# A two-block transformer kernel on one core: the first block's work in a new order, the modulation fetched and multiplied by halves

## The reference, cut to what matters

```python
mod = jax.nn.silu(c) @ w_mod[l] + b_mod[l]            # c: 1 x 1024, w_mod: 1024 x 6144
sh_m, sc_m, gt_m, sh_f, sc_f, gt_f = jnp.split(mod, 6)
h = rms_norm(x, g_mix_norm[l]) * (1.0 + sc_m) + sh_m
q_a, k_a, v_a, q_i, k_i, w_i, q_b, k_b, v_b, gate_a, gate_b = jnp.split(h @ w_in[l], split_at)
o_a = dsa_attention(q_a, k_a, v_a, q_i, k_i, w_i)     # 64 keys of each query by index scores
o_b = moba_attention(q_b, k_b, v_b)                   # causal, one block of 256
merged = sigmoid(gate_a) * (o_a @ w_br_dsa[l]) + sigmoid(gate_b) * (o_b @ w_br_moba[l])
x = x + gt_m * (merged @ w_out[l])
h = rms_norm(x, g_ffn_norm[l]) * (1.0 + sc_f) + sh_f
g_ff, u_ff = jnp.split(h @ w_gate_up[l], 2)
x = x + gt_f * ((silu(g_ff) * u_ff) @ w_down[l])
```

## Time and profile before

| | |
|---|---|
| median of three runs | 1673.88 us |
| the profiled execution's own time | 1669.84 us |
| its span | 1668.0 us |
| mean granted clock of TensorE | 0.945 |
| TensorE busy | 1498.2 us (90%) |
| DVE busy | 844.6 us (51%) |
| ACT busy | 690.7 us (41%) |
| read from HBM | 268.15 MB |
| chain that ended last: TensorE, DVE, ACT, DMA | 78%, 9%, 5%, 3% |

### The profile page before, as it was taken

How to read it: one execution, slowest core, us unless ns; L and a number is a source line. 1 busy time by engine, 2 the same in 40 slices (tenths; PEclk the granted TensorE clock), 3 DMA queues, 4 the chain that set the end, 5 groups by cost and what they waited for, 6 DMA issues and landing times.

```text
span 1668.0 us, 17947 instructions
## 1 busy us (share of the span) xinstructions
PE 1498.2 (90%) x6942; PEld 1194.7 (72%) x6942; DVE 844.6 (51%) x1011; ACT 690.7 (41%) x864; POOL 34.2 (2%) x52
## 2 busy tenths in 40 slices
PE   4989896769999999999899999799997777899998
PEld 2757664558887788877688887678885664588886
DVE  1465573545455554554755445544545336555453
ACT  2334343333433534444344444644433345553442
POOL 0010000000000000000000001000000010000000
PEclk9899998879999999999899999989999777999999
DMA  8654553535655556544456564535655230055552
GB/s 305 205 190 132 209 177 126 169 109 177 190 188 177 174 180 191 187 146 157 160 170 200 176 202 140 194 101 184 191 181 175 81 127 1 1 170 184 187 191 76
DMA packets 187879, 270.10 MB, mean 162 GB/s; under 512 B 8350, under 2 KB 134118, under 8 KB 187816
## 3 DMA queue, kind: packets, MB, share of 16 engines
q1 hardware_dynamic: 186660, 267.08, 48.8%
q10 hardware_dynamic: 996, 1.88, 0.3%
q0 software_dynamic: 160, 0.26, 0.2%
HBM read 268.15 MB, written 1.05 MB: 161 GB/s over the span
## 4 chain that ended last, share of the span: by engine, by line
PE 78%; DVE 9%; ACT 5%; DMA 3%; issue 3%; SPq 0%; POOL 0%; POOLq 0%; ACTq 0%; DVEq 0%
PE bank L1561 23%; PE bank L1563 23%; PE bank L1562 23%; DVE w_lo_ring L1125 2%; DMA raw_ring<-in_w_in_dram 2%; ACT w_hi_ring L832 2%; PE bank L1591 2%; PE bank L1695 1%; PE bank L1663 1%; PE bank L1748 1%; DVE arena L1413 1%; DMA glu_s<-in_cmp_pos_dram 1%; DMA raw_ring<-in_w_br_moba_dram 1%; PE bank L1824 1%; DVE arena L1397 1%
## 5 line engine op out<-in xcount | busy, mean ns | idle before, releaser
L1125 DVE TENSOR_TENSOR w_lo_ring<-raw_ring,w_hi_ring 128x2048 fp32r<-128x2048 f32 (+1 forms) x231 | 525.4, 2277 | 548.3 <-ACT w_hi_ring L1081 361.4
L1561 PE MATMUL bank<-w_hi_ring,h_hi 128*128 128x512 f32 (+2 forms) x1392 | 560.1, 402 | 2.7 <-issue 2.2
L1563 PE MATMUL bank<-w_hi_ring,h_lo 128*128 128x512 f32 (+2 forms) x1392 | 548.2, 394 | 0.0
L1562 PE MATMUL bank<-w_lo_ring,h_hi 128*128 128x512 f32 (+2 forms) x1392 | 547.9, 394 | 0.0
L1081 ACT ACTIVATE w_hi_ring<-raw_ring 128x2048 fp32r<-128x2048 f32 x158 | 302.5, 1915 | 322.4 <-PE bank L1563 320.2
L1561 PEld LDWEIGHTS bank<-w_hi_ring,h_hi 128*128 128x128 f32 x1392 | 270.0, 194 | 66.1 <-issue 13.1
L1563 PEld LDWEIGHTS bank<-w_hi_ring,h_lo 128*128 128x128 f32 x1392 | 268.2, 193 | 56.4
L1562 PEld LDWEIGHTS bank<-w_lo_ring,h_hi 128*128 128x128 f32 x1392 | 269.5, 194 | 51.3
L832 ACT ACTIVATE w_hi_ring<-raw_ring 128x2048 fp32r<-128x2048 f32 (+1 forms) x73 | 136.5, 1876 | 180.8 <-PE bank L1563 113.5
L1561 PE MATMUL bank<-w_hi_ring,f_hi 128*128 128x512 f32 x440 | 171.9, 391 | 7.5 <-DVE f_lo L1519 7.5
L1563 PE MATMUL bank<-w_hi_ring,f_lo 128*128 128x512 f32 x440 | 171.5, 390 | 0.0
(11 more groups left out here) (228 smaller groups left out, 877.3 us busy)
## 6 DMA issues: line engine op xcount, KB each, us to landing
raw_ring<-in_ffn_w_gate_up_dram SPq DMA_DIRECT2D x176, 512.0 KB
raw_ring<-in_ffn_w_down_dram SPq DMA_DIRECT2D x44, 1024.0 KB
raw_ring<-in_w_in_dram SPq DMA_DIRECT2D x22, 1024.0 KB
raw_ring<-in_w_gate_up_dram SPq DMA_DIRECT2D x44, 512.0 KB
raw_ring<-in_w_mod_dram SPq DMA_DIRECT2D x18, 1024.0 KB
raw_ring<-in_w_down_dram SPq DMA_DIRECT2D x11, 1024.0 KB
raw_ring<-in_conv_w_in_dram SPq DMA_DIRECT2D x16, 512.0 KB
arena<-in_w_mod_dram SPq DMA_DIRECT2D x6, 1024.0 KB, 16.0
```

The costliest lines, as they stand in the source:

```text
L1125: dve.tensor_tensor(w_lo[:, u % RING, 0:words], raw[:, r % RING, 0:words], w_hi[:, u % RING, 0:words].bitcast(F32), ALU.subtract).then_inc ...
L1561: pe.matmul(dst, hi, whi, start=start, stop=False)
L1562: pe.matmul(dst, hi, wlo, start=False, stop=False)
L1563: return pe.matmul(dst, lo, whi, start=False, stop=stop)
```

## The change

Nothing of the computation is left out. The plan's items stand in a new order, and some are cut in two:

- *Modulation by halves.* A half row is an item of its own (`mod_row(m, half)`): TensorE multiplies one half into one bank, ACT copies the first half to `acc`, DVE adds the second to it (a new instruction). The two halves are fetched and multiplied around one unit, so that a unit, a half, a unit and a half follow each other in the ring, and a half frees its slot when TensorE has done it. The sum stands right behind the second half.
- *h in two halves.* Chunks 2 and 0 (halves of scale and shift for tiles 0 to 3) come first, `mod_a` works by halves, and unit 0 (qi, first half) runs before chunks 3 and 1 are multiplied. The gain rows are issued by ACT's queue behind x.
- *Evacuations behind their units.* Most of them stand right behind the unit that ends the product, where they stood behind the next unit. ki comes after qi. Index products are inside three units instead of two.
- *Dsa's attention in three units instead of four*, with half of the transposes of o ahead of gb's last unit, and the sigmoid behind the others.
- *moba's branch first, products by chunk*: bb 0, ba 0, bb 1, ba 1 (moba's output stands in tiles 0 to 3 now); the first half of merged is transposed before ba 1, whose unit is done one tile of tokens after the other (`by_token_tile`), the second half inside out1. out1's last unit is done that way too.
- *Mod chunk 11 at the end*: it is fetched during out1 and multiplied behind it, before x is scaled; the four `normf` groups and unit 31 (first of the feed-forward) are interleaved.

```diff
+    def by_token_tile(stage, chunk, number, parts, between=()):
+        u = len(units)
+        units.append((stage, chunk, number))
+        for tt in range(TT):
+            add("lin", stage=stage, chunk=chunk, part=number, parts=parts, unit=u, sub=tt, subs=TT, by_tt=True)
+            add("evac", stage=stage, chunk=chunk, tt=tt)
+            if tt == 0:
+                plan.extend(between)
+        add("then split", unit=u)
...
-    part("qa", 0, 0, 2, [evac("ga", 1), mod_row(7), topk(0, 2), topk(0, 3)])
-    part("qa", 0, 1, 2, [mod_sum(7), mod_load(8), topk(1, 0)])
+    part("qa", 0, 0, 2, [mod_row(7, 0), mod(7, 1), topk(1, 0)])
+    part("qa", 0, 1, 2, [mod_row(7, 1), mod_sum(7), evac("qa"), mod(8, 0)])
...
+    part("out1", 1, 0, 2, [mod(11, 1)])
+    by_token_tile("out1", 1, 1, 2)
+    add("square")
+    plan.extend(mod_rows(11) + mod_sum(11))
+    add("scale_x", norm=1)
...
+    def transfer(*entry):
+        r = number("early") if entry[0] == "mod" and entry[1] in EARLY_MODS else EARLY + number("ring")
+        raw[r] = entry
+        issue.append(r)
+        return r
...
+    freed = {r: ("raw_done", e[1] + 1) if e[0] == "unit" else ("t_done", find["tg", "mrow", (e[2], e[1])] + 1) for r, e in raw.items()}
...
+                    if st == "mrow" and item["c"]:
+                        dve.wait_ge(sem("t_done"), tg + 1)
+                        wait_group(dve, find["tg", "mrow", (0, g)])
+                        a = acc[:, item["of"] % 2, :]
+                        dve.tensor_tensor(a, b[:, :], a, ALU.add).then_inc(free, 1)
...
                     elif st == "mod":
-                        wait_group(pe, find["tg", "mrow", g])
+                        wait_group(pe, find["tg", "mrow", (1, g)])
```

More of the change, by code:

```diff
@@ L124, in lin_out @@
         units.append((stage, 1, 0))
[L125 to L132, removed]
+        by_token_tile(stage, 1, 1, 2, between=tgroup("norm", 2, norm=then))
     def nsa_attention():
@@ L231, in make_plan @@
-    add("mod_a", norm=0)
+    plan.extend(mod_rows(0) + mod_sum(0))
+    add("mod_a", norm=0, half=0)
+    plan.extend(tgroup("normf", 4, norm=0)[:2])
     add("then split", unit=-RING)
-    plan.extend(tgroup("normf", 2, norm=0))
-    add("then split", unit=1 - RING)
-    plan.extend(tgroup("normf", 4, norm=0)[2:])
[L236 to L244, removed]
+    plan.extend(mod_load(3) + mod_load(1))
+    add("lin", stage="qi", chunk=0, part=0, parts=2, unit=0, sub=0, subs=1)
+    units.append(("qi", 0, 0))
+    plan.extend(mod_rows(3) + mod_sum(3) + mod_rows(1) + mod_sum(1))
@@ new lines, in make_plan @@
+    add("mod_a", norm=0, half=1)
+    plan.extend(tgroup("normf", 4, norm=0)[2:])
+    add("then split", unit=3 - RING)
+    part("qi", 0, 1, 2, [evac("qi"), mod(4, 0)])
+    part("ki", 0, 0, 1, [mod_row(4, 0), evac("ki"), mod(4, 1)])
+    part("qb", 0, 0, 2, [mod_row(4, 1), mod_sum(4), tgroup("ki", 1), mod(5, 0)])
+    part("qb", 0, 1, 2, [tgroup("qi", 2), evac("qb"), mod_row(5, 0), mod(5, 1)])
+    part("kb", 0, 0, 2, [mod_row(5, 1), mod_sum(5), mod(6, 0)])
+    part("kb", 0, 1, 2, [tgroup("qb", 2), evac("kb"), mod_row(6, 0), mod(6, 1)], [index[0], [], index[1], index[2]])
@@ L270, in make_plan @@
-    plan.extend(evac("bb", 1))
-    add("mod_a", norm=1)
-    plan.extend(tgroup("merged", 4))
-    for c in range(2):
-        lin("out1", c, 2)
-    norm(1, False)
-    ffn(0, "f0", 1, then=2)
+    part("ga", 0, 0, 2, [topk(0, 0)], inside[0])
+    part("ga", 0, 1, 2, [evac("ga"), topk(0, 1)], inside[1])
+    part("ga", 1, 0, 2, [topk(0, 2)], inside[2])
+    part("ga", 1, 1, 2, [evac("ga", 1), topk(0, 3), mod(7, 0)], inside[3])
+    part("qa", 0, 0, 2, [mod_row(7, 0), mod(7, 1), topk(1, 0)])
+    part("qa", 0, 1, 2, [mod_row(7, 1), mod_sum(7), evac("qa"), mod(8, 0)])
@@ new lines, in make_plan @@
+    part("gb", 1, 0, 2, [tgroup("o", 4)[:2]], inside[2])
+    part("gb", 1, 1, 2, [evac("gb", 1), tgroup("o", 4)[2:]])
+    add("sigmoid")
+    part("bb", 0, 0, 1, [mod(10, 0)])
+    part("ba", 0, 0, 1, [evac("bb", 0), mod_row(10, 0), mod(10, 1)])
+    part("bb", 1, 0, 1, [evac("ba", 0), mod_row(10, 1), mod_sum(10), evac("bb", 1), tgroup("merged", 4)[:2]])
+    add("mod_a", norm=1, half=0)
+    by_token_tile("ba", 1, 0, 1)
+    part("out1", 0, 0, 2, inside=[tgroup("merged", 4)[2:], []])
+    part("out1", 0, 1, 2, [evac("out1", 0), mod(11, 0)])
@@ L277, in make_plan @@
+    part("out1", 1, 0, 2, [mod(11, 1)])
[3 more added lines that the diff above has]
+    add("scale_x", norm=1)
+    plan.extend(tgroup("normf", 4, norm=1)[:2])
+    add("gu", unit=len(units), sub=0)
+    plan.extend(tgroup("normf", 4, norm=1)[2:])
+    add("gu", unit=len(units), sub=1)
+    units.extend([("f0", 0, 0), ("f0", 0, 1)])
+    ffn(0, "f0", 1, then=2, begun=True)
     begin_glu("f1", 2)
@@ L331, in make_plan @@
     for item in plan:
-        if item["kind"] == "lin" and item["unit"] == 0:
-            split(RING - 1)
         if item["kind"] == "then split":
@@ L444, in two_block_program @@
 def two_block_program(nc, A, out):
[L445 removed]
+    plan, units, raws, issue, unit_raw, find, pair_after, freed = make_plan()
     def rows(w):
```

168 lines of the change are left out of this document (75 added, 93 removed).

## The result

The changed kernel takes 1680.07 us (median of 11 runs, 1674.39 to 1682.87) against 1673.88 for the kernel before (11 runs, 1669.98 to 1676.51): 0.35% slower, ratio 1.0035 with a 95% interval of 1.0023 to 1.0047. The forecast was 1673.5, no change; the measured time lies 6.6 above it, at the upper edge of the forecast's own stretch of 1667 to 1680.

What follows compares the result with a forecast made beforehand. TensorE, busy for 90% of the span, was taken as the bound, so only its waits and low clock could be won back. Terms summed to -0.4 us on the profiled 1669.84, 4.0 below the median: 1673.5, range 1659 to 1687.

Steps and rivals of the forecast that it cites:

- both mechanisms that were to eat the gain: Mod-row sums wait for adds behind low splits (+3.9, +4.9); updates after out1 wait behind a split needing row 11 (+10.4).
- dsa: Attention in three units instead of four: same matmuls with the waits nearer, +0.2 us, bounds -2 and +4.
- start to ki's end: From the start through ki: unit 0 starts earlier, at 31.7 instead of 36.3, then loses its lead; +1.9 us.
- units 3 to 8: Half mod rows make sums wait for adds behind low splits, with some lower clock: 19.9 against 16.0, +3.9 us.
- moba: The moba attention stretch keeps its places: 0 us.
- the next six units: The six units after moba: waits for adds in front of sums, 14.2 against 9.3, +4.9 us.
- o transposes to the end of out1: Waits behind the sigmoid and for merged go, new waits of 9.3 come, mod row 11 moves out: -21.7 us.
- end of out1 to the second unit: Out1's end to the second feed-forward unit: updates wait behind a split whose transfer needs row 11's first half; +10.4 us.
- rival 2: The low clock lasts behind waits for sums, each costing 5 to 6 instead of 2.5: 11 more, 1684.5 us; 15%.
- Rival 3: The start gains nothing: shared rings land the gain rows at 16.1 again, unit 0 at 36.3; +4.6, 1678.1 us; 8%.
- row 6 is the exception: Mod row 6 meets the index scores: kb's rope and unit 9's split stand ahead of index product 3 on DVE; 7.3 us.
- Rival 1: DVE reaches each add a microsecond earlier, so waits stay short and the clock up: 13 less, 1660 us; 27%.

Runs made afterwards that it cites:

- e3_rows_sp: The changed kernel with the seven small transfers of gains back on SP behind the first two 1 MB transfers: 1682.65 us, 1.0046 against the kernel before.
- e2_tail: The changed kernel with mod row 11's halves and sum and the splits of units 32 and 33 rearranged around out1's end: 1665.64 us.
- e6_dsa4: e4_both with dsa's attention over four units instead of three and the four o transposes behind the last: 1639.83 us, 0.9794 against the kernel before.
- e5_before_sig: The kernel before with only the sigmoid moved behind the o copies: 1669.54 us, 0.9976 against the kernel before.
- e4_both: The changed kernel with the sums of mod rows 4 to 10 one unit later, plus e2_tail's edits: 1648.55 us, 0.9852 against the kernel before.
- e7_tail2: e4_both with row 11's sum behind the first gate_up unit's first half and unit 33's split behind the first two norm transposes: 1648.45 us.
- e6_again: The kernel of e6_dsa4 run a second time, as control on the same chip: 1641.22 us, 0.9798 against the kernel before.

## Why the prediction was wrong

Wrong was the size, and with it the sign: both mechanisms that were to eat the gain are there, where the prediction put them, and each was undone by itself. The steps that failed are three terms of the sum: dsa in three units, taken as free; the lower clock in the stretches up to moba, priced too low; and the start, where transfers that set the pace were left out. They carry 9.5 of the 10.4 us between forecast and profile.

How firm each size is can be read from two more profiles: e3_rows_sp differs from the changed kernel only in the gains' transfers (and so in the first term), e2_tail only from out1's third unit on. Both are divided at the same places:

| term | forecast | changed kernel | e2_tail | e3_rows_sp |
|---|---|---|---|---|
| start to ki's end | +1.9 | +3.4 | +6.4 | +7.7 |
| units 3 to 8 | +3.9 | +8.1 | +3.9 | +6.8 |
| moba | 0 | -0.9 | -0.9 | -0.9 |
| the next six units | +4.9 | +4.3 | +4.6 | +7.6 |
| dsa | +0.2 | +4.0 | +4.5 | +3.1 |
| o transposes to the end of out1 | -21.7 | -20.5 | | -20.4 |
| end of out1 to the second unit | +10.4 | +11.7 | | +11.6 |

```profile
71.49:144.74 73.25, 62.15 (x267) 38.94 (x267) 39.37 (x75) 24.22 (x41) 4.87 (x5) 0.87 0.54 187
72.80:149.02 76.22, 65.05 (x266) 40.17 (x267) 40.79 (x75) 24.11 (x41) 4.87 (x5) 0.83 0.52 179
```

The two rows are units 3 to 8 in e2_tail and in e3_rows_sp.

*dsa, +0.2, measured +4.0 (+3.1 to +4.5).* This was the worst step: "the same matmuls with the waits nearer". The bound of +4 was right and the value taken was not. A split stands on ACT and DVE ahead of a softmax step at each unit's end; with fewer TensorE units between them it is not hidden (3.21 us). I counted 4.5 us of waits, the trace has 6.7 and 1.5 more of lower clock. e6_dsa4 gave it back.

*Start and units 3 to 8, +5.8 together, measured +11.5.* How the excess is shared between the two differs from profile to profile, but the two together come to +10.3 in e2_tail and +14.5 in e3_rows_sp, of which some 2 are that run's own edit. In units 3 to 8 of the changed kernel the waits were about right: TensorE was idle for 77.49 - 65.29 = 12.2 us, and before for 69.38 - 58.93 = 10.5. What failed is the price of the clock: TensorE was busy for 6.4 us more with as many matmuls (x267), at a mean clock of 0.82 instead of 0.90, and I had allowed for one or two stretches of 2 us per wait. Behind waits of 2.55, 1.30 and 0.91 us between 123 and 134 us it was 0.50 until 141; in e2_tail, behind 2.47, 1.82 and 1.20, from 132 to 139. So rival 2, the low clock that lasts, came true in part, in this one place. It named 1684.5 as the end, which was 4.4 too much. In e2_tail units 3 to 8 cost just the 3.9 of the forecast, but there the clock had already fallen inside ki, and ki ended 3.0 later. The forecast had put ki at full clock (5.2 us); it took 5.4 in the changed kernel and 7.5 in e2_tail. The last section shows this.

At the start itself the gains landed at 9.3, better than the 11.5 that I took. But unit 0 began at 34.0 instead of 31.7, because the sum went on from the rows as if nothing else were late: next on the path were the 1 MB transfers of mod row 0, the last of them in at 22.3. Rival 3 (no gain) did not come true; e3_rows_sp shows 1.3 to 2.3 us of gain at unit 0. The Trainium skill (DMA: Bandwidth & Descriptors, Issuing engines are not separate DMA queues) is not against it: it speaks of shared engines, not of one shared ring as rival 3 did. ACT issued the seven between 1.24 and 4.03 us, behind x and while SP issued four megabytes; in e3_rows_sp SP issued them between 2.99 and 6.06, behind two. They were issued some 2 us later there and landed 6.8 later. Whether it was the other queue or the earlier place that counted, no run here tells apart.

*The end, +10.4, measured +11.7; o transposes to out1, -21.7, measured -20.5; the next six, +4.9, measured +4.3; moba, 0, measured -0.9.* These steps held, the next six with a profile (e3_rows_sp) that gives 7.6. So did the claims that the add comes right behind a low split, that row 6 is the exception, and that nothing behind 400 us moves. The wait for the high split in front of the updates was to be seen, and was 15.6 us long. Of the 20.5, the part put down to the sigmoid alone (9.1 and 1.7 of clock) was too large for it: e5_before_sig gives 4.1. The other 16 us or so were not taken apart: 3.9 is mod row 11, moved out by design, and what the order of the branches, the splits and gb's evacuation each give is argued from waits that are gone, not shown by a run.

Rival 1 (short waits, clock up) asked for adds a microsecond earlier; in the changed kernel the waits were within 0.6 us of the 3.5 and 4.1 forecast for rows 4, 5, 7 and 10, and of the 2.5 for 8 and 9 too (1.54, with 1.00 and 1.15 us ahead of the half row itself, for the copies of the transposes). Only row 4's is not firm: 3.41 here, but 1.57 in e2_tail and 1.80 in e3_rows_sp, where TensorE ran the unit ahead of it at the lower clock and came to the sum later.

Last, the sum was made against a profiled execution that was 4.0 us below its median; adding the 4.0 assumed that the changed kernel's would be as lucky. It was at its median, so 10.3 between the profiles became 6.2 between the medians. That is luck. Where it lies is known in part: e5_before_sig has the old order up to the o transposes, and its profile reached the end of qi 2.5 us later and the o transposes 1.9 later. One slip in the arithmetic of the prediction changes nothing: seven lags shorter by 0.6 us make the sum -4.6, not -4.

## What to carry to other kernels

When a row is worked in halves, look at what the second half's add stands behind on its own engine: an add of 0.7 us behind a split that waits for a transfer is ready when the transfer is, and a reader of it (the sum) belongs one unit further on. A split placed ahead of an evacuation should not wait for a ring slot that is freed only behind that evacuation's unit. Both were visible in the written order; moving the two places, with dsa's spread and the first splits, turned a kernel 0.35% slower into one 2.5% faster. And a term read from one pair of profiles can be several microseconds of luck: units 3 to 8 gave +8.1, +3.9 and +6.8 in three profiles of the same order.

## What the runs showed of the hardware

The clock can fall while TensorE is busy. Windows of e2_tail inside ki (48 narrow products, 128x72, from 63.96 to 71.5), and the same place in the changed kernel, whose order is the same up to there:

```profile
64.80:66.80 2.00, 2.00 (x21) 2.00 (x20) 1.49 (x4) 2.00 (x2) 0.00 (x0) 1.00 0.93 339
66.80:68.80 2.00, 2.00 (x13) 2.00 (x12) 1.93 (x5) 0.24 (x1) 0.00 (x0) 0.54 0.00 0
```

```profile
64.00:66.00 2.00, 2.00 (x20) 2.00 (x19) 1.63 (x4) 2.00 (x2) 0.00 (x0) 1.00 0.94 344
66.00:68.00 2.00, 2.00 (x21) 2.00 (x20) 1.93 (x5) 0.10 (x1) 0.00 (x0) 1.00 0.04 9
```

TensorE is busy for the whole 2.00 us in both, and in one the granted clock goes from 1.00 to 0.54, then stays at 0.50 for some 10 us: 1.2 instead of 2.4 GHz. The stretch of unit 1 and ki took 14.5 to 14.6 us in nine of the eleven profiled executions that have this order (that of the changed kernel and of all runs but e5_before_sig), and 12.3 and 12.4 in the other two, the changed kernel's and e4_both's. With the row and unit behind it this is 5 us (57.3 to 82.3 in e7_tail2 against 56.8 to 76.8 in e4_both). So the changed kernel's profile was a lucky one in this place, though not on the whole.

In the kernel before ki comes first, and its 0.50 from 44 to 54 is another case: it was there from ki's first products at 42.18.

```profile
42.00:44.00 2.00, 2.00 (x12) 2.00 (x10) 1.89 (x1) 1.90 (x5) 0.00 (x0) 0.50 1.05 383
```

The waits ahead of it were of 1.93 us, which the prediction named, and of 0.41 at 41.7. That it then lasted through 10 us without a gap shows again that the lower clock can hold while TensorE is busy with narrow products. The Trainium skill (TensorE: Matmul & The Clock Gate, What's actually happening) says that activity is what releases the throttle, and that the same kernel shows a different number of slow matmuls from run to run. The second agrees with e6_dsa4 and e6_again, which are one kernel: from unit 1's start to ki's took 7.1 us in one and 8.3 in the other. The first does not explain a fall with TensorE busy for 2.00 of 2.00 us. What makes the clock fall or not inside ki, no run here shows.

One more thing to know when reading a clock column: at the very start it can be wrong. Up to 38.4 us the granted clock of the changed kernel reads 1.00, but the products of unit 0 start 0.43 us apart, as at the lower clock, and from then on 0.23. The 0.90 of that kernel's first row above is too high for this reason.
